# A sink matmul that streams 128 equal columns in place of one

## What is computed

```python
# first block, swa_sink_attention
s = s * (HEAD_DIM ** -0.5) + bias
s = jnp.where(mask[None, :, None, None], s, NEG_INF)
sink = jnp.broadcast_to(sink, s.shape[:-1] + (1,))
p = jax.nn.softmax(jnp.concatenate([s, sink], axis=-1), axis=-1)[..., :-1]
o = jnp.einsum('bnhgqk,bnkhd->bnqhgd', p.astype(v.dtype), vb)
...
# second block, windowed_attention
p = jax.nn.softmax(jnp.concatenate([sk, s_ctx, s_loc], axis=-1), axis=-1)
```

## Time and profile before

| | |
|---|---|
| time, median of 2 runs | 3197.15 us (3195.77 and 3198.53) |
| the profiled execution, first to last instruction | 3195.4 us |
| TensorE busy | 2964.9 us (93%), 12442 matmul records |
| VectorE, ScalarE, GpSimd busy | 47%, 35%, 21% |
| mean granted clock of TensorE | 0.856 of full speed |

### The profile page before, as it was taken

One profiled execution on the slowest core, in us unless ns is written; L12 is line 12 of the kernel. 1 busy time (PEld: TensorE's weight loads), 2 busy tenths in 40 slices (PEclk: granted clock), 3 DMA queues, 4 the chain that ended last, 5 costly groups with the idle time before them and its releaser, 6 DMA issues.

```text
span 3195.4 us, 35358 instructions
## 1 busy us (share of the span) xinstructions
PE 2964.9 (93%) x12442; PEld 2254.6 (71%) x12442; DVE 1516.9 (47%) x2164; ACT 1111.2 (35%) x1524; POOL 661.9 (21%) x389
## 2 busy tenths in 40 slices
PE   6998999998979999899994999999999789999995
PEld 3884666776548878777783787676778448888884
DVE  4114333663353350545306333332331589999996
ACT  3112111333223332333324111111112438888885
POOL 1220000001324456444463123000002001111110
PEclk9998555998989999999996998555559879999997
DMA  6000000001513222222231011000000489999995
GB/s 242 27 27 27 1 0 0 1 0 79 175 37 104 92 92 92 81 90 92 92 105 40 30 50 40 0 1 0 0 0 13 159 317 386 398 393 398 398 390 172
DMA packets 83595, 370.85 MB, mean 116 GB/s; under 512 B 7660, under 2 KB 8860, under 8 KB 70048
## 3 DMA queue, kind: packets, MB, share of 16 engines
q1 hardware_dynamic: 78912, 352.92, 29.2%
q0 software_dynamic: 4608, 16.91, 2.0%
HBM read 348.73 MB, written 21.05 MB: 116 GB/s over the span
## 4 chain that ended last, share of the span: by engine, by line
PE 81%; issue 7%; DVE 6%; POOL 3%; ACT 2%; DMA 1%; SPq 0%; ACTq 0%; POOLq 0%; DVEq 0%
PE ps L828 9%; PE ps L829 9%; PE ps L830 9%; PE ps L658 7%; PE ps L1080 5%; PE ps L1082 5%; PE ps L1081 5%; PE ps L650 4%; PE ps L985 3%; POOL w_lo L2019 3%; PE ps L990 2%; PE ps L780 2%; PE ps L779 2%; PE ps L798 2%; PE ps L769 2%
## 5 line engine op out<-in xcount | busy, mean ns | idle before, releaser
L2019 POOL TENSOR_TENSOR w_lo<-arena,w_hi 128x1024 fp32r<-128x1024 f32 x166 | 399.2, 2405 | 910.9 <-ACT w_hi L1274 910.8
L1924 DVE TENSOR_TENSOR e_lo<-arena,e_hi 128x1024 fp32r<-128x1024 f32 x384 | 453.0, 1221 | 36.2 <-ACT e_hi L1453 23.8
L1453 ACT ACTIVATE e_hi<-arena 128x1024 fp32r<-128x1024 f32 x384 | 403.7, 1061 | 102.9 <-PE ps L1082 102.0
L1247 ACT ACTIVATE arena<-ps,tiny 128x257 f32<-128x257 f32 (+5 forms) x192 | 126.2, 657 | 683.1 <-DVE tiny L1636 681.4
L1274 ACT ACTIVATE w_hi<-arena 128x1024 fp32r<-128x1024 f32 x166 | 175.0, 1055 | 460.9 <-PE ps L830 460.8
L1636 DVE TENSOR_REDUCE tiny<-ps 128x1 f32<-128x257 f32 (+5 forms) x192 | 125.3, 653 | 353.1 <-PE ps L769 323.7
L828 PE MATMUL ps<-h_hi,w_hi 128*128 128x512 f32 x704 | 277.8, 395 | 15.6 <-POOL w_lo L2019 11.7
L830 PE MATMUL ps<-h_hi,w_lo 128*128 128x512 f32 x704 | 275.5, 391 | 0.0
L829 PE MATMUL ps<-h_lo,w_hi 128*128 128x512 f32 x704 | 275.4, 391 | 0.0
L658 PEld LDWEIGHTS ps<-arena 128*128 128x128 f32 x1424 | 266.4, 277 | 0.0
L658 PE MATMUL ps<-arena 128*128 (+1 forms) x1424 | 265.1, 350 | 0.0
(11 more groups left out here) (303 smaller groups left out, 5373.9 us busy)
## 6 DMA issues: line engine op xcount, KB each, us to landing
arena<-in_w_up SPq DMA_DIRECT2D x108, 1024.0 KB, 7.4
arena<-in_w_down SPq DMA_DIRECT2D x86, 1024.0 KB, 9.7
arena<-in_w_gate SPq DMA_DIRECT2D x64, 1024.0 KB, 11.4
arena<-in_w_in SPq DMA_DIRECT2D x15, 1024.0 KB, 4.8
arena<-in_w_ada SPq DMA_DIRECT2D x12, 1024.0 KB, 12.2
arena<-in_w_ada SPq DMA_DIRECT2D x16, 768.0 KB, 5.5
arena<-in_w_out SPq DMA_DIRECT2D x8, 1024.0 KB, 4.8
routed_rows<-arena SPq DMA_DIRECT2D x8, 520.0 KB, 2.6
```

Of the source, the lines that this page charges most:

```text
L1453: act_e.activation(e_hi[:, (2 * sl + a) % RING, :], slot[sl][:, a * D:(a + 1) * D], ACT.Copy).then_inc(s_ehi, 1)
L1924: v.tensor_tensor(e_lo[:, r, :], slot[sl][:, a * D:(a + 1) * D], e_hi[:, r, :].bitcast(F32), ALU.subtract).then_inc(s_elo, 1)
L2019: gp.tensor_tensor(w_lo[:, q, :], slot[c][:, q * D:(q + 1) * D], w_hi[:, q, :].bitcast(F32), ALU.subtract).then_inc(s_wlo, 1)
```

## The change

The moving operand of the sink is read 128 times over, so that the matmul writes 128 equal columns, from the one behind the scores on. VectorE and ScalarE read the scores and the first of these columns, as before. In the first block the columns end at 256 or 384 of the bank's 512; in the second they stand at 256 to 383 of the bank of the context scores. No other instruction, and no wait, is changed; on every engine the instructions stand in the same order as before. Lines behind the function move down by one.

```diff
             def sink(u, layer, b, at):
 
-                return pe.matmul(ps[:, b, at:at + 1], con("mean")[0:1, :], sinkB[0:1, layer, u // 2 + 4 * (u % 2):u // 2 + 4 * (u % 2) + 1], start=True, stop=True)
+                h = u // 2 + 4 * (u % 2)
+                return pe.matmul(ps[:, b, at:at + P], con("mean")[0:1, :], sinkB[0:1, layer, h:h + 1].to_broadcast([1, P]), start=True, stop=True)
```

## The result

The changed kernel takes 3222.66 us (3219.57 and 3225.75), against 3197.15 before: a ratio of 1.008, 95% interval 1.005 to 1.0109. Timed again in six runs beside eleven of the kernel before, it takes 3220.87 us against 3196.82, ratio 1.0083 (1.0066 to 1.010). The forecast was 3223.

A forecast was written before the change was run, and what follows sets the result against it. TensorE, busy for 93% of the span, was taken to bound the kernel. Sinks add 25.8 us at low clock and 0.6 at full, 26.4 in all: 3195.4 to 3221.8, plus 1.75 to the runs' median, predicted 3223 us, range 3209 to 3243.

The forecast's parts named there:

- What bounds: Both attention stages with a sink: TensorE's queue is full, no matmul waits for another engine, so added time lengthens each period.
- The price, 0.21 us at the low clock: Each low-clock sink holds TensorE's queue for 0.72 us instead of 0.51; at full clock the increase is 0.11 us.
- the rows with 64 and 128 rows of contraction: Profile records L779 and L780, first stage, low clock: float32 products of 128 columns, both 0.72 us, taken for one row too.
- The explanation of the price: At the sink, two weight loads hide the first half of the 128-column stream, so the increase is 0.21 us.
- the half slope: In L780, 128 further columns cost 0.44 us (0.72 to 1.16); from 1 to 128 columns costs half of that.
- The sum: Over both stages' sinks: 123 units at 0.21 us plus 5 at 0.11, 26.4 us, all on TensorE's queue.
- The clock: Granted clock stays at 0.50 in the slow part of both attention stages despite the added columns.
- The rows of few-row matmuls: Two stretches behind the attention: 16-row streaming had clock 0.50, transposes over all 128 rows had 1.00.
- The clock's: Rival: added columns hold the full clock in the attention stages; 2950 us for both, 3049 for the second alone; 7%.
- the ratio 0.58: A 128-column product takes 0.42 us at full clock against 0.72 at low; used to price whole units at full clock.
- The slow address: Rival: columns read from one address stream at half pace, sink 0.65 us longer, 80 us more, 3277 us; 5%.
- the sink that costs nothing: Rival: the queue hides the sink's stream behind the following transposes' weight loads; time stays at 3197 to 3205 us; 4%.

## Why the prediction was right

*What bounds.* Right: in both stages TensorE's queue has no hole and no other engine is waited for, so that each 0.21 us on it became 0.21 us of period (4.18 to 4.39, 6.85 to 7.05).

*The price, 0.21 us at the low clock.* Right to the hundredth (0.51 to 0.72), and 0.10 where 0.11 stood at the full clock. Taking it from the rows with 64 and 128 rows of contraction was sound for this sink: at the low clock, with 1, 32, 64 and 128 rows, 128 columns cost 0.72 us. That the rows make no difference is not general. The 128-row product it was read from stands behind one with 64 rows; at the full clock a 128-row sink of 128 columns behind a 128-row product holds the queue for 0.22 us (381.60 to 381.82 in the kernel with 128 rows and 128 columns) and the one-row sink for 0.41.

*The explanation of the price.* Wrong. The prediction read the half slope as the two weight loads hiding the first half of the stream. Then 64 columns should have been free, and they cost 0.10 us a unit and 15 us in all. What is hidden differs between the two passes: from 64 to 128 columns the first pass grows and the second does not. Why the passes differ, no run shows. The total at 128 came out right since it was read from a row with 128 columns and not worked out from the explanation.

*The sum.* 26.4 us were forecast; 25.5 and 24.1 us were measured. The trace gives 12.9 + 12.3 us to the two stages. The 3.9 us between them are a matter of single executions.

*The clock.* Right that it stays, and right in what counted against the rival: 128, 256 and, with 32 rows, 128 columns leave it at 0.50; 128 rows lift it, with 64 or 128 columns in every execution and with one column in the three that have a profile. What the rows do is not told apart from the closer packing that they bring: with 128 rows the sink's load starts under the bias product, and with 32 rows it waits for its end as with one (346.09, where the product starts at 344.94). The rows of few-row matmuls pointed there. The Trainium skill's rule (TensorE: Matmul & The Clock Gate, Part 1: The HAM clock gate), that sustained activity releases the low clock, is not what the trace shows if activity is read as a busy engine: 320.00 of 320.00 us busy, at 0.50.

*The rivals.* The clock's was mispriced: 2950 us was forecast for both stages, and where it came up the time was 2876 to 2901. A unit of the first stage was to take 2.55 us; it takes 2.32 with the one-row sink of one column, and 2.09 with 128 rows and 128 columns (381.06 to 383.15 in the kernel that has them). One reason is the ratio 0.58, which is that of a product of 128 columns: the products of 256 columns, over half of the unit, go from 1.16 us to 0.62 (380.74 to 381.36), a ratio of 0.54. The other is that the weight load of a 128-row sink runs under the bias product. The prediction also priced 53 units with 256 keys, the number of waits in a window; there are 64 - 8 = 56. The slow address was refuted, and so was the sink that costs nothing.

## What to carry to other kernels

Read what a small matmul costs from the distance to the next start, in a row with the same number of columns and the same clock, and not from its duration or from an explanation. Where a stage is full of TensorE records and its granted clock is low, look at the rows of contraction of its small matmuls before adding columns: a constant that is summed over one row can as well be spread over all 128, at the same value, and here, with 64 or 128 columns, that gave 10% where 128 columns on one row cost 0.8%. Look at the head of such a stage first, since the clock was lost there and, once held there, held through the rest.

## What the hardware showed that was not expected

- The granted clock went with the rows of contraction of one small matmul per unit: 0.50 with 1 or 32 rows and 128 columns, and with 1 row and 256 columns (3221 to 3275 us); 1.00 with 128 rows and 64 or 128 columns (2880 to 2885 us). Whether it is the rows themselves or the earlier weight loads that come with them, no run tells.
- With 128 rows and one column it was 1.00 in both stages in the three executions with a profile; of seven timed, four took 2876 to 2881 us and three 3062 to 3066. Why one column is at times not enough stays open; the mean clock of the three points to the second stage.
- A weight load of 128 rows started 0.32 us into a two-pass product of 128 rows; a load of one row waited for its end, 0.62 us, and so did a load of 128 rows behind a product of 64. At the full clock a one-row sink makes a unit 0.28 us longer where it stands behind 128 rows (2.32 against 2.04) and 0.09 where it stands behind 64 (3.75 against 3.66).
- A moving or stationary operand that is read from one address 128 times costs as much as one from 128 addresses (3220.87 and 3220.66 us).
